# A two-layer transformer kernel: half of the value projection and two output tiles laid between the units of the first attention

## What is computed

```python
def mixer_a(h, w_in, q_g, k_g, kidx_g, w_out, t5_bias):
    q, k, v, qi, ki, wi = jnp.split(h @ w_in, ...)        # 16 heads of 64
    # q, k: normed per head; qi, ki, wi: an index score, of which
    # lax.top_k keeps 128 of the allowed keys for each query
    logits = q k^T * 64 ** -0.5 + t5_bias[bucket(key - query)]
    p = jax.nn.softmax(logits, axis=-1)                   # over the kept keys
    return (p @ v) @ w_out                                # w_out 1024x1024
```

## Time and profile before

| | us |
|---|---|
| median of 3 runs | 1251.47 |
| profiled execution, its own time | 1252.3 |
| its span, first to last instruction | 1250.4 |
| TensorE matmuls busy | 1215.3 (97%) |
| VectorE busy | 763.2 (61%) |
| ScalarE busy | 545.9 (44%) |
| GpSimd busy | 216.5 (17%) |
| mean granted TensorE clock | 0.996 |

### The profile page before, as it was taken

How to read it: one execution, slowest core, us unless ns; L and a number is a source line. 1 busy time by engine, 2 the same in 40 slices (tenths; PEclk the granted TensorE clock), 3 DMA queues, 4 the chain that set the end, 5 groups by cost and what they waited for, 6 DMA issues and landing times.

```text
span 1250.4 us, 17161 instructions
## 1 busy us (share of the span) xinstructions
PE 1215.3 (97%) x6052; PEld 971.6 (78%) x6052; DVE 763.2 (61%) x1315; ACT 545.9 (44%) x931; POOL 216.5 (17%) x262
## 2 busy tenths in 40 slices
PE   7999999999999999999999878999999999999998
PEld 5758876678788888878888766778788888887887
DVE  4588976646766565663337778763775656664334
ACT  5554345645534343333226676643543433343222
POOL 4423433411200000000004663430400000000000
PEclk9999999999999999999999999999999999999999
DMA  6522222212322222212233100012322222212323
GB/s 234 192 93 87 83 78 60 69 51 101 108 101 94 101 101 101 84 61 91 101 101 105 50 20 1 1 35 101 130 73 101 101 101 101 90 62 84 101 92 110
DMA packets 25120, 110.83 MB, mean 89 GB/s; under 512 B 2752, under 2 KB 3136, under 8 KB 17776
## 3 DMA queue, kind: packets, MB, share of 16 engines
q1 hardware_dynamic: 25072, 110.21, 25.5%
HBM read 108.06 MB, written 6.33 MB: 91 GB/s over the span
## 4 chain that ended last, share of the span: by engine, by line
PE 88%; DVE 6%; POOL 2%; issue 2%; ACT 2%; DMA 1%; SPq 0%; DVEq 0%; POOLq 0%; ACTq 0%
PE ps L1737 25%; PE ps L1739 24%; PE ps L1738 24%; PE ps L1498 3%; PE ps L1517 3%; PE ps L1388 2%; PE ps L1376 2%; DVE h_lo L954 1%; DVE xT L1151 1%; DVE w_lo L948 1%; PE ps L1371 1%; PE ps L1482 1%; PE ps L1410 1%; PE ps L1709 1%; POOL rope_tmp L490 1%
## 5 line engine op out<-in xcount | busy, mean ns | idle before, releaser
L948 DVE TENSOR_TENSOR w_lo<-raw,w_hi 128x1024 fp32r<-128x1024 f32 (+4 forms) x114 | 195.2, 1712 | 260.9 <-ACT w_hi L582 260.9
L1737 PE MATMUL ps<-h_hi,w_hi 128*128 128x512 f32 (+1 forms) x712 | 278.6, 391 | 2.5 <-DVE w_lo L948 2.5
L582 ACT ACTIVATE w_hi<-raw 128x1024 fp32r<-128x1024 f32 (+4 forms) x124 | 177.8, 1434 | 230.3 <-PE ps L1739 230.3
L1738 PE MATMUL ps<-h_lo,w_hi 128*128 128x512 f32 (+1 forms) x712 | 277.8, 390 | 0.0
L1739 PE MATMUL ps<-h_hi,w_lo 128*128 128x512 f32 (+1 forms) x712 | 277.8, 390 | 0.0
L1737 PE MATMUL ps<-a_hi,w_hi 128*128 128x512 f32 x480 | 188.0, 392 | 2.1 <-DVE w_lo L948 1.6
L1738 PE MATMUL ps<-a_lo,w_hi 128*128 128x512 f32 x480 | 186.8, 389 | 0.0
L1739 PE MATMUL ps<-a_hi,w_lo 128*128 128x512 f32 x480 | 186.8, 389 | 0.0
L1737 PEld LDWEIGHTS ps<-h_hi,w_hi 128*128 128x128 f32 (+1 forms) x712 | 133.6, 188 | 32.1 <-DVE w_lo L948 3.4
L1738 PEld LDWEIGHTS ps<-h_lo,w_hi 128*128 128x128 f32 (+1 forms) x712 | 133.7, 188 | 28.3 <-issue 0.6
L1739 PEld LDWEIGHTS ps<-h_hi,w_lo 128*128 128x128 f32 (+1 forms) x712 | 133.5, 188 | 28.4 <-issue 0.7
(11 more groups left out here) (188 smaller groups left out, 1510.7 us busy)
## 6 DMA issues: line engine op xcount, KB each, us to landing
raw<-in_f_up SPq DMA_DIRECT2D x44, 1024.0 KB, 4.8
raw<-in_f_w_down SPq DMA_DIRECT2D x44, 512.0 KB, 3.3
raw<-in_a_in_wide SPq DMA_DIRECT2D x13, 1024.0 KB, 4.8
bias_tiles<-bias_rows SPq DMA_DIRECT2D x1, 4096.0 KB, 19.7
raw<-in_a_w_out SPq DMA_DIRECT2D x8, 512.0 KB, 3.2
raw<-in_b_w_out SPq DMA_DIRECT2D x8, 512.0 KB, 3.3
xT<-in_xt SPq DMA_DIRECT2D x4, 512.0 KB, 6.5
toep_b<-bias_tiles SPq DMA_DIRECT2D x8, 256.0 KB, 3.2
```

The lines of the kernel that those rows point to most:

```text
L582: sc.activation(w_hi[:, s, 0:n], raw[:, s, 0:n], ACT.Copy).then_inc(w_hi_done, 1)
L948: dve.tensor_tensor(w_lo[:, s, 0:n], raw[:, s, 0:n], w_hi[:, s, 0:n].bitcast(F32), ALU.subtract)\
L1737: pe.matmul(dst, s_hi, m_hi, start=start, stop=False)
L1738: pe.matmul(dst, s_hi, m_lo, start=False, stop=False)
```

## The change

- **Values.** Chunk 7 is taken out of the loop over chunks. Before attention TensorE does the first four `product3` of token tiles 0 and 1 (24 matmuls), scores 0 and 1, the last four of tile 0, scores 2, and the last four of tile 1. Tiles 2 and 3 are laid between the units: at steps 0 to 9, after `turn(s)`, two or one `product3`.
- **Output tiles.** Tiles 0 and 1 of `w_out` (`EARLY_TILES`) are multiplied at steps 12 to 19 (`part_product(d)`, 6 matmuls for one output block `d`), into bank 6 (`FILL_BANK`). VectorE adds each result to `xT` at the step that follows, after its `turned_probs`. `early_rows` and `onto_residual` then begin with tile 2.
- **Banks.** `turn` has two banks (4 and 5, one for each head of the pair) in the first attention.
- **Homes.** `h_hi` and `h_lo` must live until step 9, so in the first attention `probs`, `probsT` and the bias tiles move to `act` and `qT`. The bias tiles load after the first half of chunk 6. The tiles of `w_out` get places of 1024 columns in both halves of the slots (`out_place`).

```diff
+def out_place(k):
+    return ((0, 0), (0, D), (1, 0), (1, D), (0, 0), (1, 0), (0, 0), (1, 0))[k]
-def turn_bank(u, e):
-    return 4 + (2 * u + e) % 3
+def turn_bank(n, u, e):
+    return 4 + ((2 * u + e) % 3 if n else e)
+FILL_BANK = 6
+EARLY_TILES = 2
+FILL_AT = 12
+V_LAST = len(A_CHUNKS) - 1
...
+        probs = [[act[:, 16 + 2 * j:18 + 2 * j] for j in range(4)], probs_b]
+        probsT = [[qT[:, 8 + 2 * j:10 + 2 * j] for j in range(2)], turned_b]
+        toep = [[rope_tmp[:].rearrange("p a n -> p (a n)"), qT[:, 12]], [qT[:, 13], qT[:, 14]]]
...
@@ SP
-            sp.wait_ge(pa_half, len(A_CHUNKS))
+            sp.wait_ge(pa_half, V_LAST)
+            for i in range(2):
+                for e in range(2):
+                    load_toep(i, e)
+            load_out(0)
+            load_out(1)
...
+                if i == 5:
+                    load_out(2)
+                    load_out(3)
+            for k in range(4, KD):
+                load_out(k)
@@ ScalarE
+            def last_values(t):
+                sc.wait_ge(pa_done, rows_done(V_LAST, t))
+                sc.activation(v[:, t, 512:1024], ps[:, FILL_BANK + (t == 1), :], ACT.Identity,
+                              scale=rstd[:, t:t + 1]).then_inc(v_free, 1)
...
+                if c == V_LAST:
                     table(ACT.Exp)
                     exps(0, 0, 0)
                     exps(0, 0, 1)
+                    last_values(0)
+                    exps(0, 1, 0)
+                    exps(0, 1, 1)
+                    last_values(1)
+                    break
...
+                    if n == 0:
+                        if FILL_AT - 2 <= s < FILL_AT - 2 + EARLY_TILES:
+                            kk = s - (FILL_AT - 2)
+                            out_hi(kk, (pa_done, rows_done(V_LAST, T - 1)))
+                            sc.activation(part_hi[:, kk, :], act[:, kk, :], ACT.Copy).then_inc(part_hi_ok, 1)
+                        if s in (FILL_AT + 1, FILL_AT + 3):
+                            out_hi(2 + s // 2 - FILL_AT // 2)
+                        if s in (UNITS - 5, UNITS - 4):
+                            act_hi(0, s - UNITS + 7, s % 2 == 0, True)
+                        if s == UNITS - 2:
+                            out_hi(4, (part_mm, KD))
...
+                    if n == 0 and s in (4, 9):
+                        last_values(2 + s // 5)
...
+                if n == 0:
+                    act_hi(0, 4, 0, False)
+                    out_hi(5, (r_used[0], 1))
+                    act_hi(0, 5, 1, False)
@@ VectorE, attention(n)
                 for s in range(UNITS):
                     if s + 1 < UNITS:
                         inverse_sums(n, s + 1)
+                    if n == 0 and s in (UNITS - 4, UNITS - 3):
+                        act_lo(0, s - UNITS + 6, s % 2)
                     for e in range(2):
                         if not out_by_scalar(s, e):
                             turned_probs(n, s, e)
+                    if n == 0 and FILL_AT < s <= FILL_AT + KD:
+                        d = s - FILL_AT - 1
+                        dve.wait_ge(part_mm, d + 1)
+                        dve.tensor_tensor(xT[:, d, :], xT[:, d, :], ps[:, FILL_BANK, :], ALU.add)\
+                            .then_inc(part_out, 1)
                     if s + 3 < UNITS:
                         logits(n, s + 3)
+                    if n == 0:
+                        if FILL_AT - 2 <= s < FILL_AT - 2 + EARLY_TILES:
+                            kk = s - (FILL_AT - 2)
+                            out_lo(kk)
+                            dve.wait_ge(part_hi_ok, kk + 1)
+                            dve.tensor_tensor(part_lo[:, kk, :], act[:, kk, :], part_hi[:, kk, :].bitcast(F32),
+                                              ALU.subtract).then_inc(part_lo_ok, 1)
+                        if s in (FILL_AT + 1, FILL_AT + 3):
+                            out_lo(2 + s // 2 - FILL_AT // 2)
+                        if s == UNITS - 2:
+                            out_lo(4)
@@ TensorE
+            pe.wait_ge(w_lo_done, U_A + 2 * V_LAST + 1)
+            for t in range(2):
+                pe.wait_ge(tp_out, 4 * T + 1 - QI_FROM + t + 3)
+                last_values(t, range(0, 4))
+            pe.wait_ge(v_free, T)
+            scores(0, 0)
+            scores(0, 1)
+            pe.wait_ge(w_lo_done, U_AOUT)
+            last_values(0, range(4, KD))
+            scores(0, 2)
+            last_values(1, range(4, KD))
...
             def turn(n, u):
...
-                    if 2 * u + e >= 3:
-                        before = divmod(2 * u + e - 3, 2)
+                    if 2 * u + e >= (3 if n else 2):
+                        before = divmod(2 * u + e - 3, 2) if n else (u - 1, e)
                         pe.wait_ge((pt_act if out_by_scalar(*before) else pt_dve)[n], outs_before(*before))
...
+            def part_product(d):
+                pe.wait_ge(w_lo_done, U_AOUT + EARLY_TILES)
+                pe.wait_ge(part_lo_ok, EARLY_TILES)
+                if d:
+                    pe.wait_ge(part_out, d)
+                for k in range(EARLY_TILES):
+                    s, at = out_place(k)
+                    cols = slice(at + d * P, at + (d + 1) * P)
+                    ins = product3(pe, ps[:, FILL_BANK, :], w_hi[:, s, cols], w_lo[:, s, cols], part_hi[:, k, :],
+                                   part_lo[:, k, :], k == 0, k == EARLY_TILES - 1)
+                ins.then_inc(part_mm, 1)
...
             def attention(n):
                 for s in range(UNITS):
                     turn(n, s)
+                    if n == 0 and s < 10:
+                        t, j = 2 + s // 5, s % 5
+                        if j == 0:
+                            pe.wait_ge(v_free, T + (1, 3)[t - 2])
+                        last_values(t, ((0, 1), (2,), (3, 4), (5,), (6, 7))[j])
+                    if n == 0 and FILL_AT <= s < FILL_AT + KD:
+                        part_product(s - FILL_AT)
                     if s + 3 < UNITS:
                         scores(n, s + 3)
```

More of the change, by code:

```diff
@@ L244, in hybrid_layers_kernel @@
             kv_lo = sb("kv_lo", [P, D], F32R, scope)
[L245 to L253, removed]
+        with ExitStack() as scope:
+            part_hi = sb("part_hi", [P, EARLY_TILES, S], F32R, scope)
+            part_lo = sb("part_lo", [P, EARLY_TILES, S], F32R, scope)
+        probs_b = [sb(f"probs{j}", [P, 2, S]) for j in range(4)]
+        sb("pad_h0", [P, 4, S])
+        turned_b = [sb(f"probsT{j}", [P, 2, S]) for j in range(2)]
         with ExitStack() as scope:
             qT = sb("qT", [P, 16, S], F32, scope)
+        probs = [[act[:, 16 + 2 * j:18 + 2 * j] for j in range(4)], probs_b]
+        probsT = [[qT[:, 8 + 2 * j:10 + 2 * j] for j in range(2)], turned_b]
+        toep = [[rope_tmp[:].rearrange("p a n -> p (a n)"), qT[:, 12]], [qT[:, 13], qT[:, 14]]]
         a_hi = sb("a_hi", [P, 2, S], F32R)
@@ L705, in _ @@
                         sc.wait_ge(pa_done, rows_done(c, t))
-                        bank = t if c == 6 else 4 + t
-                        sc.activation(v[:, t, (c - 6) * 512:(c - 5) * 512], ps[:, bank, :], ACT.Identity,
+                        sc.activation(v[:, t, 0:512], ps[:, t, :], ACT.Identity,
                                       scale=rstd[:, t:t + 1]).then_inc(v_free, 1)
-                        if c == len(A_CHUNKS) - 1 and t < 2:
-                            exps(0, 1, t)
                     if 3 <= c <= 6:
                         turned_out(A_CHUNKS[c - 1][2], (c - 1) % 2, t)
-                if c not in (2, len(A_CHUNKS) - 1):
+                if c != 2:
                     hi(U_A + 2 * c + 3, (pa_done, rows_done(c, T - 1)))
@@ L742, in act_hi, with out_hi @@
                 if not first:
-                    sc.wait_ge(r_used[n], kk - 1)
+                    sc.wait_ge(r_used[n], kk - 1 - (0 if n else EARLY_TILES))
                 sc.activation(a_hi[:, b, :], act[:, kk, :], ACT.Copy).then_inc(r_hi[n], 1)
+            def out_hi(k, free=None):
+                s, at = out_place(k)
+                sc.wait_ge(w_raw[k % 2], 8 * (U_AOUT + k - k % 2) + 16)
+                if free is not None:
+                    sc.wait_ge(*free)
+                sc.activation(w_hi[:, s, at:at + D], raw[:, s, at:at + D], ACT.Copy).then_inc(w_hi_done, 1)
             def attention(n):
@@ L1082, in _ @@
                 topk_done += TOPK_AMONG.get(c, 0)
[L1083 to L1089 removed]
+                lo(U_A + 2 * c + 3)
                 if c == 2:
@@ L1548, in attention, with out_rows @@
                 mix(n, UNITS - 1)
+            def out_rows():
+                for k in range(EARLY_TILES, KD - 2):
+                    early = k < EARLY_TILES + 2
+                    if not early:
+                        pe.wait_ge(w_lo_done, U_AOUT + k + 1)
+                        pe.wait_ge(r_lo[0], k + 1 - EARLY_TILES)
+                    for d in (4, 5, 6, 7) if early else range(KD):
+                        if k == EARLY_TILES and d == 4:
```

(7 more changed lines are left out.)

163 lines of the change are left out of this document (96 added, 67 removed).

## The result

| | before | after |
|---|---|---|
| median of 4 runs each, us | 1251.63 | 1268.16 |
| lowest to highest | 1250.41 to 1252.01 | 1266.70 to 1271.21 |
| profiled execution, its own time | 1252.3 | 1271.21 |
| its span | 1250.4 | 1269.4 |

The ratio is 1.0135, with a 95% interval of 1.0122 to 1.0147: slower by 16.5 us, where +15.6 was forecast. The profiled execution of after is its slowest one, so its own parts have to be read against 1271.21, not against the median.

The account below looks back on a forecast made before the run. The prediction took a full TensorE, with no holes to fill, as the bound. Its terms, 2.0 + 2.0 + 12.1 − 0.45, gave +15.6 us on the profiled 1252.3, a forecast median of 1267.0 us, range 1261 to 1272.

Parts of the forecast that it names:

- What bounds the kernel: Whole kernel, mainly values and attention: TensorE is full without holes, so the change can only make holes.
- Steps 13 to 19: Early output products in attention: each waits for VectorE's add, queued behind this step's transposes and copies; +12.1 us, bounds 0 to 16.
- Steps 10 to 12: Attention before the first output product: TensorE waits for low parts and ScalarE's late copy; +2.0 us, bounds 0 to 3.5.
- Switching: At 18 new insertions in attention, the first product after another kind of matmul costs 0.11 us more; +2.0, bounds 0 to 4.
- Start of attention and steps 0 to 9: First scores and value products between units: TensorE gets no new wait; 0 us.
- End: Output projection after attention: its first remaining tile has weights already converted, so TensorE no longer waits for them; −0.45 us.
- The clock: TensorE's clock during the waits in attention: short idle gaps keep it at 1.00; 0 us.
- rival B: Clock also falls at the longest waits, about 1.5 us each: 1270 for two falls, 1279 at every wait; chance 12%.
- A: Output products in attention: VectorE's adds are in time, so their waits vanish; 1255.0 us, or 1253.0; chance 7%.
- C: Attention has slack inside busy TensorE, so fills cost under half of 0.23 us a matmul; faster, 1245.5 us; chance 4%.

Follow-up runs that it names:

- values alone: Changed kernel without early output tiles (no part products or adds; all eight tiles after attention), value products still between units: 1251.72 us, 1.0002 of before.
- all three: Changed kernel with add at its product's step, part products at steps 13 to 20, weight low parts of tiles 2 and 3 before logits: 1252.01 us.
- the first experiment: Changed kernel with VectorE's add of each block moved one step earlier, into the step of its product, before the logits: 1254.11 us, 1.0019 of before.
- product last: Changed kernel with the early output product moved to the end of TensorE's step, after scores and mix; VectorE unchanged: 1252.90 us, 1.0014 of before.
- the longer link: Changed kernel with one more VectorE operation, the block's maximum with itself, ahead of each of the eight adds: 1277.65 us, 1.0210 of before.
- low parts ahead: Changed kernel with VectorE making weight low parts of output tiles 2 and 3 before its logits at steps 13 and 15: 1267.69 us, 1.0133 of before.

## Why the prediction was right, point by point

**What bounds the kernel.** Right. TensorE was full and could only lose time. The values alone and the kernel with all three edits are the test: with half of the fills in the attention and no wait, and with all of them and only the small wait for GpSimd, 1251.72 and 1252.01 against 1251.59 and 1251.97.

**Steps 13 to 19, +12.1.** Right in its mechanism and nearly in its size. From the start of a `turn` to the start of the product, less 0.63 us for a `turn` of six and 0.85 for one of eight (the unwaited distances in the first experiment, 235.41 to 236.04 and 239.59 to 240.44):

| step | predicted distance | measured | unwaited | wait |
|---|---|---|---|---|
| 13 | 2.26 | 2.35 | 0.63 | 1.72 |
| 14 | 2.93 | 2.99 | 0.85 | 2.14 |
| 15 | 2.41 | 2.45 | 0.63 | 1.82 |
| 16 | 3.21 | 3.24 | 0.63 | 2.61 |
| 17 | 2.03 | 2.12 | 0.85 | 1.27 |
| 18 | 2.41 | 2.45 | 0.63 | 1.82 |
| 19 | 2.26 | 2.34 | 0.63 | 1.71 |

(The predicted distance is the wait of the prediction plus its 0.71 or 0.93 for the `turn`.) The chain as predicted is short by 0.03 to 0.09 us a step. The waits sum to 13.1 us. The waits view has 11.4 for the same seven, 0.24 less for each: the idle time is counted from the modelled end of the last transpose, and that lies beyond the point where the next matmul could have started (0.87 us for a record whose slot is 0.63).

**Steps 10 to 12, +2.0.** Right. The product of step 12 starts 232.49 − 229.87 = 2.62 us after its `turn`, 2.0 more than unwaited. The 0.5 of it that the prediction gave to ScalarE's late copy was a wait for GpSimd's scaled unit. Its idle row says 0.27, but in the kernel with all three the `turn` of step 12, with the same row of 0.27, takes 231.12 − 229.96 = 1.16 us where a `turn` of six takes 0.71: 0.45. The values alone, which make no parts of the activations at steps 10 and 11, do not have this wait. Moving the first product takes only the wait for `part_lo` away, 2.0 − 0.45 = 1.55; by the stages below it was 1.25 with the product last and 1.45 with all three, so 0.1 to 0.3 us is not accounted for.

**Switching, +2.0.** This is the term that was mis-sized. The first product does take 0.31 to 0.34 us, but beside a `turn` the way into it is shorter: the slot of six transposes is 0.63, not 0.71, and of eight 0.85, not 0.93. The prediction took the price of entering from one row and did not ask what the group before it would gain. Step 3 with its three products takes 198.49 − 194.77 = 3.72 us; the unit of the same shape took 3.00, and three products at 0.23 are 0.69. That leaves 0.03. In the first experiment step 13 takes 239.59 − 235.41 = 4.18 with six products; without them such a unit is 0.71 + 1.27 + 0.81 = 2.79, and six at 0.23 are 1.38: 0.01; step 14, in the same way, leaves 0.04. So 18 insertions cost 0.2 to 0.7 us, near 0.5. What this term had too much, 1.5, was in part missing in the waits, which came out 1.0 longer: a shorter slot of the `turn` is a longer wait behind it, 0.08 for each of seven, and the chain itself is longer by the 0.03 to 0.09 above. That the two errors nearly cancel is luck.

**Start of attention and steps 0 to 9, 0.** Right: TensorE has no wait there in any of the profiles.

**End, −0.45.** Right: −0.35 by the stage with the values alone, which also holds ten switches.

**The clock, 0.** Right in one of the three profiles that hold these waits, wrong in the one of the changed kernel (0.94 from 228 to 281 us, 0.96 from 195 to 285; the prediction had set 0.95 for the stage as its bound, and which side of it this is depends on where the stage is cut) and in the one of the longer link (0.83 from 230 to 240 us, 0.84 from 250 to 260). Here are TensorE's granted clock and busy time in two stretches (us, busy PE, clock, DMA share, GB/s), after:

```profile
234.00:237.00 3.00, 3.00 (x16) 0.55 0.59 213
246.00:250.00 4.00, 3.02 (x7) 0.62 0.01 4
```

and a longer stretch of the kernel with the low parts ahead, which has waits of 1.03 to 1.57 us in the same seven steps:

```profile
227.00:277.00 50.00, 38.80 (x280) 1.00 0.19 64
```

In after's profile the clock is near its lower level, 1.2 of 2.4 GHz, twice: behind the waits of step 12 (1.30 and 0.27 us) and of step 14 (1.90). In its timeline the pitch of the products changes in mid-group:

```profile
233.26 0.59 PE L1893 MATMUL ps<-part_hi,w_hi 128*128 128x512 f32 x1
233.64 0.63 PE L1894 MATMUL ps<-part_lo,w_hi 128*128 128x512 f32 x1
234.07 0.63 PE L1895 MATMUL ps<-part_hi,w_lo 128*128 128x512 f32 x1
```

From 233.64 to 234.07 it is 0.43 us, where 0.23 is usual. From product to next `turn` that step takes 237.84 − 232.49 = 5.35 us; the same work took 235.41 − 231.63 = 3.78 in the first experiment. The fall cost 1.57 us. The second cost 252.15 − 246.73 = 5.42 less 244.33 − 240.44 = 3.89, 1.53 us. The price is the 1.5 us of rival B, and its mechanism is real, but not in every profile: with the add in the step of its product the same wait at step 12 left the clock at 1.00. Nor does the longest wait decide: behind the one of 2.37 us at step 16 the products kept their pitch. Nor does the distance from `turn` to product: 2.62 and 2.99 us ahead of the two falls, 3.24 at step 16 without one. The rule of the Trainium skill that the prediction cited (TensorE: Matmul & The Clock Gate, "HAM oscillation — how this bites in real kernels"), as it was read there, that short idle gaps keep the clock, is not borne out by this profile.

**The sum.** The stages, in which the second layer's own changes of clock do not count:

| kernel | stage, us | over before |
|---|---|---|
| before | 147.21 | |
| after | 165.45 | +18.2, of it 3.1 for the clock |
| add in its product's step | 149.29 | +2.1 |
| product last | 148.04 | +0.8 |
| values alone | 146.86 | −0.35 |
| low parts ahead | 160.62 | +13.4 |
| all three | 315.69 − 167.85 = 147.84 | +0.6 |

Waits for `xT` 13.1, step 12 2.0 (0.45 of it for GpSimd), switching near 0.5, end −0.45: 15.2, and after shows 18.2 − 3.1 = 15.1. Without waits for `xT` the same sum gives 2.1, as measured. With the low parts ahead after's waits are less by 1.8, which gives 13.3 against 13.4. On 1251.6 the 15.1 give 1266.7, the fastest run of after; its other runs lie 1.4, 1.6 and 4.5 us above it, at mean clocks of 0.996, 0.995 and 0.993 against its 0.997. If the median holds about one fall that the forecast did not count, the mis-sized switching made up for a part of it: 1267.0 against 1268.16. That the unprofiled runs owe their distance to falls in this stage is argued from their clocks, not seen: the kernel before has none there, and its 25 runs still spread from 1250.16 to 1254.27, at mean clocks of 1.000 to 0.996. Falls in the second layer could make up the same distance.

**Rivals.** A (the adds are in time) fell with the first line of the waits view, and its number, 1255.0, is close to what the first experiment measured when it made it true: 1254.11. B is right in kind: with two falls it said 1270, and the profiled run of after, which has two, took 1271.21. They lay behind steps 12 and 14, not 14 and 16 as B had it. C fell with the values alone: a fill costs its 0.23 us a matmul, not half of it. The rule of the Trainium skill (Perfetto Trace Analysis, "Identifying the Most-Contended Engine") that spoke for C points the wrong way here: weight loads were busy for 66% of the attention, and there was still no room. The times from start to start in the timeline said so.

## What stays open

What decides whether the clock falls behind these waits. Nothing was run on that alone, and each kernel has one profile. A second bank for the early output tiles, which should open the chain with the add left in its place, was not run either. Nor was it followed where the last 0.1 to 0.3 us of the step-12 term sit.

## What to carry to other kernels

When a product gets a single bank beside a pipelined loop, ask of the instruction that empties it what stands ahead of it in its engine's order: an operation whose data were ready a step earlier still comes last if it is written behind copies of this step's results. Moved one step earlier, ahead of them, it made TensorE wait for nothing here, and behind them for 13 us, with VectorE idle 30% of the time. And work moved into a stretch is only worth something if that stretch has gaps from start to start: 48 matmuls moved from one full stretch to another made no difference (1251.72 against 1251.59 us).

## What the runs showed of the hardware that was not expected

- A group of transposes with a product behind it takes 0.08 us less to the next start (0.63 and 0.85 us for six and eight, against 0.71 and 0.93 with scores behind it). That nearly pays for the slow first product, and laying products between transposes and scores is all but free.
- The maximum of a 128x512 block with itself, written in place, took VectorE 0.68 to 0.72 us in four of eight cases and 0.92 to 0.95 in the other four; the adds behind it took 0.69 each time. What makes the difference was not followed.
- The clock fell behind waits of 1.3, 1.9 and 2.6 us in some profiles and held behind others of 1.0 to 2.9 us, at 1.53 to 1.57 us for each fall that was worked out. Without a wait of this kind there was no fall in the attention.
- The idle time of TensorE's rows understates a wait behind transposes by about 0.24 us, as the record of the transposes reaches past the point where the next matmul can start.
